# A two-layer mixture-of-experts decoder step: an earlier load for one expert of the first layer, and an expert's down products placed behind the next expert's gate and up products

## What is computed

```python
N_GROUPS = 4; EXPERTS_PER_GROUP = 8; TOP_K_IN_GROUP = 2     # 32 experts
D_MODEL = 1024; D_FF_EXPERT = 512

# hier_moe(x, ...): each token goes to the two best experts of its best group
hid = jax.nn.silu(xb @ w_gate[e]) * (xb @ w_up[e])
y = hid @ w_down[e]                     # weighted and added to the token's row
```

## Time and profile before

| | |
|---|---|
| time, median of 3 runs | 1859.22 us (1856.38 to 1862.15) |
| time of the profiled execution | 1855.08 us |
| its span, first to last instruction | 1853.4 us |
| PE busy | 1672.0 us, 90% of the span |
| DMA packets | 515.60 MB, mean 278 GB/s |
| mean granted clock of PE | 0.931 of full speed |

### The profile page before, as it was taken

The page is one execution under the profiler, slowest core; times in us unless marked ns, Lnnn a source line. Parts: engine busy times, 40 slices in busy tenths (PEclk is TensorE's granted clock), DMA queues, the critical chain, the costliest instruction groups (busy, mean ns, idle before and its releaser), DMA issues.

```text
span 1853.4 us, 27694 instructions
## 1 busy us (share of the span) xinstructions
PE 1672.0 (90%) x9306; PEld 874.9 (47%) x9307; DVE 541.4 (29%) x1490; ACT 420.5 (23%) x888; POOL 247.8 (13%) x348
## 2 busy tenths in 40 slices
PE   7899899999888989898889999899898989899885
PEld 5466666655544444444434445455443434344332
DVE  2333343322421111111111656764211111111113
ACT  2233344421111111111111224341011111111112
POOL 1231024400011111111111301000111111111110
PEclk9899899999888999998999999999798989898987
DMA  5252137744489999999998800122999999999973
GB/s 180 70 153 85 50 128 251 250 160 164 172 339 405 409 411 408 405 410 408 411 411 362 308 13 6 41 112 108 360 399 412 415 412 405 403 403 406 404 329 150
DMA packets 83342, 515.60 MB, mean 278 GB/s; under 512 B 22664, under 2 KB 41049, under 8 KB 56794
## 3 DMA queue, kind: packets, MB, share of 16 engines
q1 hardware_dynamic: 61962, 461.35, 62.7%
q0 software_dynamic: 21296, 53.15, 8.7%
HBM read 506.99 MB, written 26.52 MB: 288 GB/s over the span
## 4 chain that ended last, share of the span: by engine, by line
PE 76%; DMA 7%; issue 6%; DVE 6%; ACT 3%; DVEq 1%; SPq 0%; ACTq 0%; POOLq 0%
PE ps L1923 67%; PE ps L1928 9%; DMA mem<-in_moe_w_up 5%; DVE mem L1582 1%; ACT mem L979 1%; ACT mem L735 1%; DMA mem<-moe_rows_back 1%; DVE mem L1701 0%; DMA mem<-in_cache_mla 0%; DMA mem<-in_mla_w_a 0%; DMA moe_rows_back<-mem 0%; DVE mem L1293 0%; ACT mem L906 0%; ACT mem L909 0%; DVE mem L1672 0%
## 5 line engine op out<-in xcount | busy, mean ns | idle before, releaser
L1923 PE MATMUL ps<-mem 128*64 128x512 f32 (+13 forms) x7330 | 1433.9, 493 | 100.3 <-issue 49.7
L1923 PEld LDWEIGHTS ps<-mem 128*64 128x64 f32 (+4 forms) x7330 | 646.1, 150 | 797.3 <-issue 710.4
L735 ACT ACTIVATE mem<-ps 128x512 f32<-128x512 f32 (+3 forms) x370 | 205.8, 568 | 723.0 <-PE ps L1923 526.3
L1928 PE MATMUL ps<-mem 128*128 128x128 f32 (+1 forms) x1976 | 273.4, 280 | 73.6 <-DVE mem L1582 45.7
L1928 PEld LDWEIGHTS ps<-mem 128*128 128x128 f32 (+1 forms) x1976 | 233.8, 171 | 172.6 <-issue 149.5
L1582 DVE TENSOR_TENSOR mem<-mem,ps 64x512 f32<-64x512 f32 x64 | 44.2, 690 | 471.0 <-ACT mem L979 471.0
L664 POOL DMA_INDIRECT mem<-moe_rows_in,mem x68 | 63.3, 931 | 559.6 <-issue 541.4
L1593 DVE COPY mem<-ps 64x512 f32<-64x512 f32 x64 | 44.4, 693 | 312.3 <-PE ps L1923 312.3
L674 POOL DMA_INDIRECT moe_rows_back<-mem x64 | 59.2, 925 | 355.0 <-DVE mem L1593 347.8
L979 ACT ACT_TABLE_LOAD x32 | 41.1, 1283 | 231.8 <-PE ps L1923 231.8
L979 ACT ACTIVATE mem<-ps 64x512 f32<-64x512 f32 x64 | 37.7, 589 | 199.8 <-PE ps L1923 199.4
(11 more groups left out here) (233 smaller groups left out, 459.8 us busy)
## 6 DMA issues: line engine op xcount, KB each, us to landing
mem<-in_moe_w_gate SPq DMA_DIRECT2D x64, 2048.0 KB, 17.8
mem<-in_moe_w_up SPq DMA_DIRECT2D x64, 2048.0 KB, 25.5
mem<-in_moe_w_down SPq DMA_DIRECT2D x64, 2048.0 KB, 23.5
mem<-in_cache_mla POOLq DMA_DIRECT2D x160, 160.0 KB, 4.5
mem<-in_cache_mla SPq DMA_DIRECT2D x96, 160.0 KB, 5.5
mem<-moe_rows_back SPq DMA_DIRECT2D x8, 1024.0 KB, 8.3
mem<-in_mla_wo SPq DMA_DIRECT2D x1, 4096.0 KB, 14.2
moe_rows_in<-mem POOLq DMA_DIRECT2D x8, 512.0 KB, 3.0
```

Of the source, the lines that this page charges most:

```text
L735: return act.activation(out, in_, ACT.Copy)
L1923: return pe.matmul(out, lhsT, rhs, start=start, stop=stop)
L1928: return pe.transpose(out, in_, ident[at:at + n, at:at + n])
```

## The change

There are two parts. (1) In layer 0, the slots are numbered the other way round, `(2 - e) % 3`: expert 1 uses slot 1 and expert 2 slot 0. Expert 1's three loads are issued when the last sample's attention is done (`pv_mm`), ahead of expert 0's; some buffers (`oT`, the router's scratch, one tile of `h_r`) move so that slot 1 is free then. Layer 1 keeps its slots and the order of its first loads. (2) In both layers the expert loop is skewed by half a step: PE does gate and up of expert `e + 1`, then down of expert `e`, then the transposes and numbers that belong to `e + 1`. ACT and DVE follow the same order.

```diff
+def slot_of(L, e):
+    return (e + 2 if L else 2 - e) % SLOTS
...
                 else:
+                    sp.wait_ge(sig["pv_mm"], happened("pv_mm", NB))
+                    gate_up(1, 1)
+                    down(1, 1)
                     sp.wait_ge(sig["oTs_mm"], happened("oTs_mm", 1))
                 gate_up(0, 2)
                 down(0, 2)
                 sp.wait_ge(sig[OUT_MM[L][0]], happened(*OUT_MM[L]))
                 sp.wait_ge(sig["root_ready"], happened("root_ready", ROOT_MOE[L] + TILES))
-                gate_up(1, 0)
+                into_0 = 1 if L else 2
+                gate_up(into_0, 0)
                 for b in range(2):
                     sp.wait_ge(sig[f"xn_out{b}"], landed(f"xn_out{b}", SAVES[b] * (L + 1)))
-                down(1, 0)
+                down(into_0, 0)
                 if L:
                     sp.wait_ge(sig["sel_ready"], happened("sel_ready", L + 1))
                     sp.wait_ge(sig["state_out"], landed("state_out", 2))
-                gate_up(2, 1)
-                down(2, 1)
+                    gate_up(2, 1)
+                    down(2, 1)
@@ the tensor engine @@
+                def follow(i, r):
+
+                    gate_up(i, r + 1)
+                    down(i, r)
+                    turns(i, r + 1)
+
+                gate_up(0, 0)
+                turns(0, 0)
-                with pe.Fori(0, NE // 6) as i:
+                with pe.Fori(0, (NE - 1) // 6) as i:
                     for r in range(6):
-                        expert(i, r)
-                for r in range(NE % 6):
-                    expert(NE // 6, r)
+                        follow(i, r)
+                for r in range((NE - 1) % 6):
+                    follow((NE - 1) // 6, r)
+                down(NE // 6, (NE - 1) % 6)
@@ the scalar engine @@
+                def follow(i, b):
+
+                    e = 2 * i + b
+                    silu(e + 1, 1 - b)
+                    rows_back_0(e, i, b)
+                    rows_T(e + 2, b)
@@ the vector engine @@
+                def follow(i, b):
+
+                    e = 2 * i + b
+                    hidden(e + 1, 1 - b)
+                    rows_back_1(e, i, b)
+                    hidden_T(e + 1, 1 - b)
```

More of the change, by code:

```diff
@@ L57 @@
 SLOTS = 3
-LOADS = tuple(sum((e + 2) % SLOTS == s for e in range(NE)) for s in range(SLOTS))
+LOADS = tuple(sum((2 - e) % SLOTS == s for e in range(NE)) for s in range(SLOTS))
 LOGITS = ((6, 7), (2, 4))
@@ L262, in build @@
         cT = m.take(2, TOK)
-        krT = [m.take(TOK)]
+        krT = [m.take(TOK) for _ in range(2)]
+        m.at = max(m.at, work)
         oT = m.take(H, TOK)
-        krT += [m.take(TOK)]
+        oT_end = m.at
         rowbuf = m.take(ROW)
@@ L338, in build @@
         ye = [r.take(D) for _ in range(2)]
+        assert r.at <= moe_end - 96 - P
+        r.at = moe_end - 96 - P
         lt = r.take(96)
         jrep = r.take(P)
-        router = Arena(mem, moe_at, moe_end)
-        h_r = [mem[:, slot_at[0] + (KD + T) * D:slot_at[0] + (KD + T + 1) * D] for T in range(TILES)]
+        router = Arena(mem, oT_end, moe_end - 96 - P)
         hT_l = [router.take(KD, P) for _ in range(2)]
@@ L973, in experts, with silu, rows_back_0 @@
                 copy(sg[0:BLK, :], ps[0:BLK, 5, :]).then_inc(sig["first_act"], 1)
[L974 to L983, removed]
+                def silu(e, b):
+                    act.wait_ge(sig["gu_mm"], happened("gu_mm", NE * L + e + 1))
+                    act.wait_ge(sig["hid_ready"], happened("hid_ready", NE * L + e))
+                    act.activation(sg[BLK:2 * BLK, :], ps[0:BLK, b, :], ACT.Silu).then_inc(sig["silu_ready"], 1)
+                def rows_back_0(e, i, b):
+                    act.wait_ge(sig["d_mm"], happened("d_mm", NE * L + e + 1))
+                    act.wait_ge(sig[f"scattered{b}"], landed(f"scattered{b}", STORES * L + i + 1))
+                    copy(ye[b][0:BLK, 0:FF], ps[0:BLK, 2 + b, :]).then_inc(sig["y0_ready"], 1)
+                def follow(i, b):
[3 more added lines that the diff above has]
+                    rows_T(e + 2, b)
+                silu(0, 0)
+                rows_T(1, 1)
+                with act.Fori(0, NE // 2 - 1) as i:
+                    follow(i, 0)
+                    follow(i, 1)
+                follow(NE // 2 - 1, 0)
+                rows_back_0(NE - 1, NE // 2 - 1, 1)
                 act.wait_ge(sig["lst_ready"], happened("lst_ready", L + 1))
@@ L1594, in experts @@
+                def follow(i, b):
[3 more added lines that the diff above has]
+                    hidden_T(e + 1, 1 - b)
+                hidden(0, 0)
+                hidden_T(0, 0)
+                with v.Fori(0, NE // 2 - 1) as i:
+                    follow(i, 0)
+                    follow(i, 1)
+                follow(NE // 2 - 1, 0)
+                rows_back_1(NE - 1, NE // 2 - 1, 1)
                 for b in range(2):
@@ L2333, in expert, with turns @@
                     last.then_inc(sig["gu_mm"], 1)
[L2335 removed]
+                def turns(i, r):
+                    e, b, _, _ = place(i, r)
+                    fetched_T(e + 1, 1 - b, (odd if b == 0 else even) + 3 * i + r // 2 + 1)
                     numbers(e + LOOK, 1 - b)
@@ L2343, in expert, with down @@
                     last.then_inc(sig["ht_mm"], 1)
+                def down(i, r):
+                    e, b, s, turn = place(i, r)
                     pe.wait_ge(sig[f"d{s}_in"], landed(f"d{s}_in", turn))
```

70 lines of the change are left out of this document (39 added, 31 removed).

## The result

The changed kernel takes 1862.70 us (median of 11 runs, 1857.10 to 1868.77), the kernel before, beside it, 1857.29 (11 runs, 1855.60 to 1862.15). The ratio is 1.0029 with a 95% interval of 1.0016 to 1.0043: 5.4 us slower, between 3.0 and 8.0. The forecast was 11.9 us slower, so the sign is right and the size is more than twice what was measured. By its time it comes nearest to the rival called the wash, which had 3 to 5 us on top of the kernel before.

What follows compares the result with a forecast made beforehand. The prediction took the stream of expert weights to bound the kernel, not PE. Early load 0, loop 0, heads 8.2 and tails 3.7 sum to 11.9 us on 1855.08: 1867 profiled, 1871 as median; range 1859 to 1880.

Steps and rivals of the forecast that it cites:

- the wash: Rival for heads and tails: no slow clock at the heads, landing 4.9 us, tails at lower ends; 1862 to 1864 us, chance 0.16.
- The bound: Expert stages of both layers: the weight stream from expert 3 on, 16.49 us per expert, sets the time, not PE.
- the 167 us: Rival that PE bounds the expert stages: 2.7 us times 62 experts, 167 us faster; chance rounds to 0.
- Part 1, the early load: Layer 0's start: expert 1's loads move earlier, but expert 3 still waits for expert 0's slot; price 0, no gain.
- Part 2 inside the loop: Expert loop: PE saves some 2.7 us per expert but then waits 3.6 us for weights; worth 0.
- The rival of the slow clock: Expert loop: PE's waits for weights lower its clock; if every second expert ran at 1.2 GHz, stages 45 us longer; chance 0.04.
- The heads: Start of each layer's stream: expert 3's down load is issued later, making the stream 4.1 us later per layer, together 8.2.
- The table load that leaves ACT's loop is off every path here: ACT's expert loop: moving the table load out was taken to have no effect on the time.
- the landing: Head of each layer: expert 3's down load was to land 6.1 us after issue, between 4.9 and 8.4.
- The tails: End of each layer: PE finishes later after expert 31's up weights land, 2.1 and 1.6 us, together 3.7.
- The sum: Whole kernel: 0 + 0 + 8.2 + 3.7 = 11.9 us slower.
- its first condition: Heads: the slow clock does not fall on expert 1's gate and up, 2.4 us less per layer.

Runs made afterwards that it cites:

- half loads: Half of each weight matrix loaded from expert 3 on: in the kernel before 1844.39 us (ratio 0.9931), in the changed kernel 1679.34 us (0.9039).
- SP's skewed loads: Changed kernel, SP issuing expert e+1's gate and up loads ahead of expert e's down load: 1853.40 us (0.9982); without the early load 1853.42 us (0.9985).
- the table load back: Changed kernel, ACT made to wait for expert 0's gate and up before loading its table for the first silu: 1871.00 us, ratio 1.0069.
- the tail in the old order: Changed kernel with down of expert 30 again ahead of gate and up of expert 31 on PE, ACT and DVE: 1864.82 us, ratio 1.0046.
- filler product: Changed kernel with SP's loads skewed plus unused PE products per expert: five gave 1965.37 us (ratio 1.0594), two gave 1851.92 us (0.9988).

## Where the prediction was right and where it failed

**The bound** was right. Every kernel of the table takes 425.0 to 428.5 us from expert 5's up landing to expert 31's, in the old order and in the new, 16.35 to 16.48 for each of 26 experts. The page's chain said PE, and the half loads show that the 167 us which it promised are there only when the stream is not.

**Part 1, the early load, price 0,** was right: 1.0000, and no difference on top of SP's skewed loads.

**Part 2 inside the loop, worth 0,** was right, with two things not as foreseen. PE mostly waits less than 3.6 us for each expert (0.55, 1.51, 3.90 in the rows), and fills the rest with a slower clock: groups of 12.1 to 13.3 where 10.52 was assumed. The rival of the slow clock did therefore happen in its mild form. 13.34 + 2.4 is 15.7, still under 16.4, and so nothing came of it. The Trainium skill ("TensorE: Matmul & The Clock Gate", HAM oscillation) tells of a kernel whose DMA waits throw the clock down: the trace agrees that the clock falls in this loop (0.91), and not that it costs time.

**The heads, 4.1 us each,** are where it failed. The streams end 1.0 and 1.8 us later, 2.8 and not 8.2. The step is the sentence "The table load that leaves ACT's loop is off every path here". The wait of 1.51 us in the earlier trace rows was, but for 0.2 us, that table load (with it taken out of the old order the transposes wait 0.23): it stood behind expert 0's gate and up products and delayed silu, hidden rows and transposes. Peeling expert 0's silu off the loop let the load be made at 512.19, while ACT waited. The prediction added the 1.5 us of wait and 2.4 us of slow clock to the new order as if both stayed. Both fell away in layer 0 (16.9 - 1.5 - 2.4 = 13.0 forecast without them, 12.7 measured), and in layer 1 the wait did and 1.7 us of slow clock stayed (14.3). Only the wait is the table load's doing; the slow clock comes and goes at this place without it (with the load back 10.52 in layer 0 and 13.31 in layer 1). With the table load back the kernel is at 12.8 us, beside the 11.9 of the forecast, and that closeness is in part luck: in layer 0 the slow clock is missing and the landing is longer by as much. The Trainium skill ("ScalarE: Activation LUTs", Step-by-step: what each stage is for) says that the load is placed right before the ACTIVATE that needs it. The traces agree and show what follows from it: where the wait is an instruction of its own ahead of the ACTIVATE, the load stands behind the wait, and where it is not, ahead of it.

A second step was mis-sized and hid part of this: the landing, and what follows from it. The prediction let the down load land 6.1 us after its issue in a queue that had run dry. It takes 8.0 and 9.4 (8.6 and 10.0 with the table load back). In layer 0 expert 3's up load, issued at 527.58, landed 14.1 us later, at 541.7, when the down load had been issued for 1.9 us, so that the gap is short there. In layer 1 the landing came 4.5 us later than before, as much as was forecast (4.1), out of a smaller delay of issue and a longer landing. But the stream's end is only 1.8 us later, for the stream is not late by as much as this one load. The loads behind it are issued from 0.6 us on and move at the same time: until it has landed, 3.2 MB go by (343 GB/s over 9.4 us), and it is 2.1. What the stream lost is rather what was not moved. An estimate from the 24 us of the table, at the 408 GB/s of the loop, is (356 - 343) x 24 / 408 = 0.8 and (358 - 318) x 24 / 408 = 2.4 us, beside 1.0 and 1.8 at the stream's end; with the table load back 2.2 and 4.9, beside 4.4 and 5.1. The rest is within what the streams of one order differ by from run to run between expert 5 and 31, up to 2.8 us.

**The tails, 2.1 and 1.6 us,** were about right: 2.5 and 2.1. The forecast's 17.3 us at the full clock, with 1.4 of slow clock in each layer (5.07 against 3.65 in layer 0; in layer 1 the group behind the landing takes 11.95 against 10.52), are the 18.7 measured. Of the 2.5 and 2.1 the order is then 1.2 and 0.7 (17.3 against 16.1 and 16.6) and the rest slow clock, which the kernel before has in its tails too; no run separates the two. That the order of the loads bears on the tail is seen in SP's skewed loads: with expert 31's gate and up ahead of expert 30's down in the queue, PE ends 8.5 and 6.9 us behind the last landing, sooner than before (11.2 and 11.5). The direct test, the tail in the old order, did not bring it down (19.9 and 18.8).

**The sum.** Forecast 0 + 0 + 8.2 + 3.7, measured by stage 0 + 0 + 2.8 + 4.6, where the medians give 5.4 in all. The wash nearly met the time but not by its own conditions: the landing was longer and not shorter, and the tails lay above the middle. Only its first condition held, in layer 0.

What stays open: what brings the slow clock to one head and not to the other; why the kernel with its tail in the old order, at 1.0046, is no better than the changed one (the intervals overlap), beyond the fact that there was no idle time to fill; and what moves the part between the layers by up to 6 us.

## What to carry to other kernels

When two resources both look full, let the backlog decide: if loads take ever longer from issue to landing, the stream of loads is the bound, and a gain on the engine buys nothing. Whoever reorders the consumer of a stream should reorder the loads in the same way; here that turned 5.4 us of loss into about 3 us of gain. Then compare it with the plain remedy: a table load taken out of the old loop gave the same 3 to 4 us, and the new order nothing beyond it. And look at the first iteration of a loop on its own, at what a peeled copy pulls out of it: a wait that is shown as data from another engine may be a table load two steps back.

## What the hardware showed that was not expected

Issued by SyncE into a nearly empty queue, a load of 2 MB takes 8.0 to 10.0 us to land, though in a full queue its neighbours land some 5 us apart (expert 31's up and down, 4.9 to 5.5). An estimate by the Trainium skill ("DMA: Bandwidth & Descriptors", Anatomy of one DMA), which gives 2.0 us and the bytes at 436 GB/s for transfers issued by GpSimd, is 6.8 us for 2.1 MB. The traces are 1.2 to 3.2 us above it, but these are not transfers of GpSimd and not loads alone: 2.7 and 3.2 MB moved while the two of the changed kernel were under way.

An instruction of a filler product, with 128 columns of weights, takes twice as long as one of the kernel's products with 64: five products are ten instructions, which take 4.5 us, 0.45 each, against 10.52 / 48 = 0.22. The kernel's products write the two halves of a bank's partitions in turn; whether that is the reason no run here shows.

The table load takes 1.28 us in each trace shown, and the silu starts 0.02 us behind it (528.30 + 1.28, then 529.60 in the kernel before).
